# Starting addresses of TensorE's operands in the token and weight buffers: from mixed offsets to one offset, 32 bytes past a multiple of 128

## What is computed

```python
def moe_swiglu(x, w_router, b_router, w_gate, w_up, w_down):
    ...
    for e in range(N_EXPERTS):
        y = y + gates[..., e:e + 1] * swiglu(x, w_gate[e], w_up[e], w_down[e])
...
def _conv_ffn(x, norm_g, w_up, conv_w, conv_b, w_down):
    h = _rmsnorm(x, norm_g)
    up = h @ w_up
    gate, val = up[..., :D_FF], up[..., D_FF:]
    gate = conv1d(gate, conv_w, width 3) + conv_b
    return (jax.nn.silu(gate) * val) @ w_down
```

## Time and profile before

| what | us |
|---|---|
| median of 3 runs | 2696.95 |
| lowest and highest run | 2693.68, 2701.14 |
| span of the profiled execution | 2699.8 |
| TensorE busy in it | 2554.3 |
| VectorE busy | 2032.6 |
| ScalarE busy | 1565.4 |

### The profile page before, as it was taken

One profiled execution on the slowest core, in us unless ns is written; L12 is line 12 of the kernel. 1 busy time (PEld: TensorE's weight loads), 2 busy tenths in 40 slices (PEclk: granted clock), 3 DMA queues, 4 the chain that ended last, 5 costly groups with the idle time before them and its releaser, 6 DMA issues.

```text
span 2699.8 us, 58833 instructions
## 1 busy us (share of the span) xinstructions
PE 2554.3 (95%) x25616; PEld 2366.9 (88%) x25616; DVE 2032.6 (75%) x3184; ACT 1565.4 (58%) x2516; POOL 51.1 (2%) x58
## 2 busy tenths in 40 slices
PE   7999999978878999999999999999988899999999
PEld 7779998856766899999999999999887699988999
DVE  5455547785545599999999999999866788575884
ACT  4335434473223477777777777777755566464662
POOL 0001100000000000000000000000003000000000
PEclk9889999977798999999999999999999999999999
DMA  6113442200001399999999999999833245441453
GB/s 251 57 71 118 184 176 96 99 1 4 20 5 65 108 338 356 338 354 345 342 357 341 354 336 361 337 360 342 332 115 113 72 172 185 168 179 57 179 176 121
DMA packets 83274, 538.71 MB, mean 200 GB/s; under 512 B 9488, under 2 KB 9616, under 8 KB 38976
## 3 DMA queue, kind: packets, MB, share of 16 engines
q1 hardware_dynamic: 82368, 530.68, 53.6%
q0 software_dynamic: 640, 4.19, 0.4%
HBM read 533.79 MB, written 1.05 MB: 198 GB/s over the span
## 4 chain that ended last, share of the span: by engine, by line
PE 85%; DVE 8%; ACT 4%; issue 2%; DMA 0%; DVEq 0%; ACTq 0%; SPq 0%; PEldq 0%
PE ps L568 23%; PE ps L569 23%; PE ps L570 23%; PE ps L574 1%; DVE sl L530 1%; PE ps L1425 1%; PE ps L1936 1%; PE ps L1410 1%; PE ps L1419 1%; PE ps L583 1%; PE ps L1384 1%; PE ps L806 1%; DVE xl L564 1%; ACT sh L523 1%; PE ps L2080 1%
## 5 line engine op out<-in xcount | busy, mean ns | idle before, releaser
L2163 DVE TENSOR_TENSOR sl<-ring,sh 128x1024 fp32r<-128x1024 f32 x613 | 735.3, 1220 | 29.1 <-ACT sh L2121 18.1
L2121 ACT ACTIVATE sh<-ring 128x1024 fp32r<-128x1024 f32 x613 | 630.5, 1053 | 1.9 <-DVE xl L2006 1.9
L568 PE MATMUL ps<-sh,xh 128*128 128x256 f32 (+2 forms) x2012 | 591.3, 294 | 10.3 <-DVE sl L530 9.5
L570 PE MATMUL ps<-sh,xl 128*128 128x256 f32 (+2 forms) x2012 | 571.8, 284 | 0.0
L569 PE MATMUL ps<-sl,xh 128*128 128x256 f32 (+2 forms) x2012 | 571.7, 284 | 0.0
L568 PE MATMUL ps<-xh,sh 128*128 128x256 f32 (+2 forms) x1856 | 535.4, 288 | 26.3 <-DVE sl L530 14.6
L569 PE MATMUL ps<-xl,sh 128*128 128x256 f32 (+2 forms) x1856 | 530.5, 286 | 0.0
L570 PE MATMUL ps<-xh,sl 128*128 128x256 f32 (+2 forms) x1856 | 527.3, 284 | 0.0
L530 DVE TENSOR_TENSOR sl<-ring,sh 128x1024 fp32r<-128x1024 f32 (+1 forms) x341 | 399.6, 1198 | 68.8 <-ACT sh L523 68.4
L523 ACT ACTIVATE sh<-ring 128x1024 fp32r<-128x1024 f32 (+1 forms) x341 | 338.8, 1021 | 112.4 <-PE ps L570 105.9
L568 PEld LDWEIGHTS ps<-sh,xh 128*128 128x128 f32 x2012 | 379.5, 189 | 21.3 <-DVE sl L530 4.7
(11 more groups left out here) (568 smaller groups left out, 3998.9 us busy)
## 6 DMA issues: line engine op xcount, KB each, us to landing
ring<-ws_d SPq DMA_DIRECT2D x229, 1024.0 KB, 7.1
ring<-ws_d SPq DMA_DIRECT2D x80, 1536.0 KB, 6.4
ring<-ws_d SPq DMA_DIRECT2D x225, 512.0 KB, 6.7
ring<-ws_d SPq DMA_DIRECT2D x24, 1408.0 KB, 6.0
ring<-ws_d SPq DMA_DIRECT2D x4, 1256.0 KB, 5.4
ring<-ws_d SPq DMA_DIRECT2D x2, 1088.0 KB, 4.9
scan_t<-scn_d POOLq DMA_DIRECT2D x1, 1824.0 KB, 7.4
ring<-ws_d SPq DMA_DIRECT2D x1, 1248.0 KB, 5.3
```

The costliest lines, as they stand in the source:

```text
L568: e.matmul(out, ah, bh, start=start, stop=False)
L570: return e.matmul(out, al, bh, start=False, stop=stop)
L2121: e.activation(out, raw(u)[:, a:z], ACT.Copy).then_inc(*af.on("high", u, i))
L2163: e.tensor_tensor(l, raw(u)[:, a:z], f32(h), SUB).then_inc(s_fd if i < 2 else s_fp, 1)
```

## The change

```diff
         ring = sb("ring", [128, RING, BW])
-        par_t, con_t, pos_t = sb("par", [128, np_]), sb("con", [128, nc_]), sb("pos", [128, 8], i32)
-        flag_t = sb("flag", [128, 8], i32)[:, 0:1]
+        par_t, con_t = sb("par", [128, np_]), sb("con", [128, nc_])
         xt = sb("xt", [128, 8 * T0])
         AB = 8 * T0
-        XW = AB + 112
+        XW = AB + 128
         NL = 2 * SLOTS * BW + 4 * XW
-        NA = (208 * 1024 - 512 - 4 * (RING * BW + np_ + nc_ + 16 + AB + NL)) // 4 // 16 * 16
+        NA = (208 * 1024 - 256 - 4 * (RING * BW + np_ + nc_ + 16 + AB + NL)) // 4 // 16 * 16
...
         arena = sb("arena", [128, NA])
+        pos_t = sb("pos", [128, 8], i32)
+        flag_t = sb("flag", [128, 8], i32)[:, 0:1]
```

## The result

The changed kernel takes 2723.43 us (median of 6 runs, 2708.19 to 2728.81) against 2698.69 us (6 runs, 2693.68 to 2706.03): the ratio is 1.0068, 95% interval 1.0046 to 1.0091, or some 18 us. A second set of runs gave 1.0088 [1.0059, 1.0117]. The change makes the kernel slower, by about what the slower rival gave (+19.9), and the forecast of -23.6 had the wrong sign.

A forecast was written before the change was run, and what follows sets the result against it. TensorE's matmul pitch was taken to bound the kernel. Terms of -7.6, -11.9 and -4.1 us summed to -23.6: 2699.8 became 2676.2, less 2.9 for the profiled execution, so 2673, with 8 in 10 from 2656 to 2718.

The forecast's parts named there:

- the slower rival: All 256-column triples and part of the 272-column ones: equal starts of high and low parts cost; +19.9 us, 2717, chance 0.22.
- What bounds the kernel: Whole kernel: TensorE, busy 2554.3 of 2699.8 us, sets the end, which moves with the pitch of matmuls in a triple.
- That an address matters: Trace of before: operand starts, all multiples of 32 bytes, change the pitch; the Trainium skill's rules gave 0 against -23.6 us.
- the first natural experiment: Mixture, tokens stationary: experts 1 and 3 take 126.1 us, 2 and 4 128.0; read as 8.5 ns a triple from stationary start.
- Experts, -7.6 us: Mixture: experts 0, 2, 4 and 6 become like 1, 3, 5 and 7, 1.9 us less each.
- 1400 ordinary triples, -11.9 us: Ordinary 256-column stages, 1048 with xh and 352 with conv_h moving: stationary start goes from 224 to 160, saving 8.5 ns each.
- 976 triples of 272 columns, -4.1 us: 272-column stages, 0.375 us a triple: half taken between 0 and -8.3 us, from the neighbouring widths.
- The second natural experiment: Convolved layers' two up projections: moving start shifted by 64 bytes, both 0.353 us a triple, so the shift changed nothing.
- Both: Whole kernel: the remainder gives 23.6 us and equal starts take 19.9; -4 us, 2693, chance 0.18.
- nothing: Whole kernel: something else of the two token pairs makes experts differ, and the layout doesn't matter; 2697, chance 0.12.
- more than the sum: All 256- and 272-column triples go to the quiet price and beyond; below 2657 us, chance 0.05.
- The test named as the cleanest: Convolved down projection: only its common remainder changes; from 0.359 us a triple to 0.35, or the prediction is wrong.

The follow-up runs named there:

- The maps: Kernels holding nothing of the network, running triples alone at many distances between operand starts; at 256 columns with all starts equal, 359.8 ns a triple.
- moe64: The changed kernel with the experts' tokens 16 words further in their buffers, 64 bytes from the weights by 256; ratio to before 1.0025.
- xw112: The changed kernel with the token buffers' width alone put back to 2288, all distances as before, every start 64 bytes lower by 256; ratio to before 1.0022.

## Why the prediction was wrong

- **What bounds the kernel: right.** The end moved with the pitch of matmuls in a triple, but for some 2 us of the tail and the stretches that vary anyway. VectorE and ScalarE didn't move, no wait is new, the memsets and the rest of the arena cost nothing that shows.
- **That an address matters: right.** The Trainium skill, SBUF — State Buffer, "Who interferes with whom", has two independent read ports for TensorE, one for the moving operand and one for weight loads; by that there was to be no effect. The maps measure 340 to 364 ns for one and the same triple with nothing else at work, so here the measurement decides. The same page of the Trainium skill, in its section "The DMA port swizzle", has lines of 16 bytes; they don't tell 0 from 64 bytes either, where the maps have 359.8 and 353.3 or 340.0.
- **The step that failed is the first natural experiment**: "the tokens are the stationary operand there; the moving weights start at 224 in both". From that the forecast took the stationary operand's own remainder as the cause. But with the weights fixed, a new start is a new distance too: even experts had stationary on moving (0), odd experts 192 off. The trace of before could not tell the two readings apart, since sh starts at 224 throughout; the forecast took the absolute one without pricing the relative one, by which the change brings all of them to 0/0/0, the slowest 256-column layout in the rows of before (0.359). The down projection shows it: only its common remainder changed, from 224 to 160, and ten triples take 3.60 us. So the terms of -7.6 and -11.9 us had a price, 8.5 ns, for something that gives nothing.
- **Experts, -7.6 us: +9.4 measured.** The even ones didn't come down to the odd ones; the odd ones went up, 2.1 us each, the even ones by 0.2 to 0.3.
- **1400 ordinary triples, -11.9 us: about +7.** 1048 went from 353.5 to 360.1 ns, +6.9 us; the 352 of conv_h stayed at 360.
- **976 triples of 272 columns, -4.1 us: about +2.5.** The 800 with xh went from 375.2 to 378.3 ns; the 176 of ffn_h, whose parts stay 128 apart, stayed at 375 to 376. The stretch of the table, which has most of them, grew by 1.5 and 1.8 us.
- **The second natural experiment** (the moving start moved by 64 and nothing changed) was read rightly as a row and wrongly as a rule: it was 128/0/0 against 128/64/0, 352.8 and 353.3 in the map. Many layouts lie at 353 there, so that two of them are alike says little of the others.
- **The slower rival** gave +6.3, +1.8 and +9.4, +2.4: measured +6.9, +1.0 and +8.4, +2.5. It got each part from the down projection's 0.359, the one stage of before that had the layout of after, and that is why it is right in size. Its mechanism, equality of high and low parts, is not what costs: moe64 has that equality, and its mixture is 2.8 us shorter than that of before. What costs in this change is that the other operand's start is the same too. So its size is right for a reason other than its own. Its counterargument, that even and odd experts have the same distance between their parts and still differ, was sound; it spoke for the distance between the operands.
- **Both, nothing, more than the sum**: none happened. The remainder gives nothing to weigh against.
- **The range** ended at 2718, 5 us short: it took in half of the slower case. The test named as the cleanest, the down projection's pitch, told the truth at one glance.

**Open**: why the distances set the pitch at all; why one layout has two pitches; and what makes the units of the odd experts 18 ns longer in xw112 than before at the same distances, 2 of the 4 us that its mixture didn't get back.

## What to carry to other kernels

When a trace seems to show that an operand's address matters, write down the addresses of all operands that are read at the same time, and ask of every natural experiment which differences it changes: an absolute reading and a relative one can fit the same rows and give opposite signs. Where one stage already has the layout to which all will be moved, its pitch is the best price there is; take it over a theory. For matmuls of 256 fp32r columns, try moving and stationary operands 64 bytes apart by 256, and the low stationary part 128 from the high one: of the five layouts tried with different neighbours it alone held the lowest pitch. It was shown on triples by themselves and on the experts, not on the dense layers.

## What the hardware showed that was not expected

- The pitch of a triple of matmuls at 256 columns goes from 340.0 to 364.2 ns with the distances of its operands by 256 bytes, with nothing else on the core, and is alike to 0.08 ns when all starts are moved by 32 bytes. At 128, 192 and 320 columns it doesn't move at the four distances tried (335.0, 335, 440.0); at 512 it goes from 680.4 to 706.7, in another order.
- The same instructions at the same addresses can run steadily at 340 or at 353 ns: behind two triples that start 0.09 us late each they go over from the one to the other for the next 30 us, at full clock; in another profile, behind the same delay, they don't.
- A better pitch made a wait for VectorE longer, 3.0 us for 1.4, and behind the longer one TensorE ran at 1.2 GHz for some microseconds (0.71 and 0.63 of the clock over 5.8 and 8 us), behind the shorter one at 2.4. So it was behind nine of ten waits of 3.0 to 3.8 us: such a wait mostly costs twice. Behind the 1.7 to 1.8 us of the last expert it was so in two of eleven profiles, behind 1.4 us in none.
